# Key pages between the slabs of a two-layer decoder step, scored in groups of four units

## The chip, the cores and the metric

The kernel runs on one core of one Trainium2 chip. The metric is the device time of one launch in microseconds. The kernel before was run three times.

## The reference

One inference step of a two-layer decoder for a prompt group (256 tokens) and a sample group (8 sequences, one new token each, with 2048 cached tokens in pages of 128). Per layer: one input projection, attention over the own tokens or the cache (12 heads) and over 256 memory tokens (4 heads), an output projection, a layer norm, a mixture of 16 experts, and another layer norm. All of it is in float32.

```python
def dsa_sample(q, k_new, v_new, qi, ki_new, wi, pool_k, pool_v, pool_ki, page_table, slopes):   # layer 0
    ki_all = concat(pool_ki[page_table], ki_new)
    sc = indexer_scores(qi, wi, ki_all)
    _, sel = lax.top_k(sc, 256)                      # the 256 best of 2049 positions
    return sparse_attend(q, k[sel], v[sel], pos_q, sel, slopes)

def fox_sample(q, k_new, v_new, logf_new, pool_k, pool_v, pool_lf, page_table):                 # layer 1
    c = cumsum(concat(pool_lf[page_table], logf_new))
    return fox_attend(q, all keys, all values, c)    # softmax(q k + c_q - c_k) v

def mem_attend(qm, mk, mv):                          # 4 heads, 256 memory tokens, both layers
    return softmax(qm mk^T / sqrt(128)) mv
```

The outputs are the new token rows of both groups and the new keys, values, index keys and forget gates.

## The kernel before

Tokens stand transposed: X holds 16 chunks of 128 features by 264 tokens. A **slab** (TensorE, L678 to L699) is a product of X, or of the transposed memory rows AT, with 512 weight columns: two weight units, 64 matmuls, four PSUM banks. Slabs alternate between banks 0 to 3 and 4 to 7; ScalarE copies the four banks out (`slab`, L1540), and the next slab on the same banks waits for that (`slab_copied`). A slab may have small work beside it: `beside(x)` is called after each four matmuls, x from 0 to 15. So `turn_memory` (L668) turns the 16 chunks of the memory rows, two per call from x = 1 on, through banks 4 to 7; at x = 1 it waits until the slab before has been copied, and each chunk waits until the one four before it has been copied by ScalarE (`turn_rows`, L1534). `own_rows` turns new keys and values into rows (`natural`, L701) for the outputs and, in layer 1, the forget gates; `query_blocks` (L736) spreads the sample queries.

**The ring.** Weights, cache pages and memory tokens go through six SBUF units of 2 MB (128 x 4096 floats). `plan(layer)` (L169) is the list of what is loaded in which order; SP walks it (L476), waits for each unit until its last user has freed it (`free`), and issues the DMAs. A weight unit is one DMA (L463). A key or value unit is pages: `load_pages` (L398 to L405) loads eight page numbers into registers and issues one DMA a page: in layer 0 a unit is one sequence, 16 pages of 128 KB; in layer 1 it is half a sequence, 8 pages of 256 KB. There are 8 key units in layer 0 and 16 in layer 1, and as many value units. In the plan all key units come behind all slabs, then mk (memory keys), v, mv, r (router), o (output weights).

**The keys.** VectorE turns each key unit in 32 x 32 blocks in place (`turn_keys`, L2066). TensorE then takes the products of a group of units (`sample_scores`, L906; the matmul is L925): for each key head and each 32 of its features d, for each unit, for each row quarter r, one matmul of 32 x 32 weights with the unit's 32 columns of every page. The PSUM column group is the sequence's number modulo 4, so a group of four sequences uses 16 tiles of the array, a group of two uses 8. Layer 0 has two groups of four units, layer 1 eight groups of two. A float32 matmul is two records in the trace. Behind the groups come the new key (L946), in layer 0 the mask of the top-k as a product (L939, L940), and then the memory keys (L971, L956), whose 16 turned blocks ScalarE copies one by one (`sample_scores`, L1673) with two banks between them.

**VectorE in layer 0:** `sample_topk` (L2019) does 32 rounds of MAX8 and MATCH_REPLACE8 over 2049 scores, writes the mask (L2024), then the 8 key transposes, `new_keys` (which waits for `memory_done`, set by ScalarE after the memory values), `prompt_topk` of block 0, the sample softmax, `prompt_topk` of block 1.

**ScalarE's queue** is in program order too, and it issues DMAs itself: in layer 0 the index pages (`load_ik`), in layer 1 the forget-gate pages, 128 of them, four times 32 (`load_lf`, L1912), between the copies of the first slabs:

```python
for k in range(3):
    if layer == 1 and k == 1: gate_rows(a)
    if layer == 1: load_lf(range(2 * k, 2 * k + 2))
    slab(layer, "q", k, ...)
if layer == 1:
    load_lf(range(6, NB)); slab(layer, "kv", 0, ...)
turn_rows(Ac, 4)
```

The order of slabs is q0, q1, q2 (queries), in layer 1 kv0 (keys), then kv (layer 0: keys and values; layer 1: values) with the memory rows beside it, qm (memory queries) with own rows beside it, mkv0 and mkv1 (memory keys and values, from AT), and then the last rows and the keys. After it: attention, output mixing (L1178), layer norm, experts (L1352 to L1440).

Of the kernel before, what the change touches and what calls it, by code (L numbers as in the profile page):

```python
# [28 lines left out]
ALU = mybir.AluOpType  # L29
# [38 lines left out]
IK_EARLY = 6  # L68

# [82 lines left out]
class Ring:  # L152
# [7 lines left out]
    def take(self, n_dma=1):  # L160
        s = self.n % RING
        self.n += 1
        before = self.used[s]
        self.full[s] += 16 * n_dma
        self.used[s] += 1
        return s, self.full[s], self.used[s], before


def plan(layer):  # L169

    u = []
    if layer == 0:
        u += [("x", 0, 3), ("x", 1, 1), ("x", 2, 1), ("x", 3, 1), ("kiwi", 0, 1)]
        u += [("qi", k, 1) for k in range(2)] + [("ln", 0, 4)] + [("qi", k, 1) for k in range(2, 4)] + [("ik", 0, 16 * (NB - IK_EARLY))]
    else:
        u += [("f", 0, 1)]
    u += [("q", k, 2 if layer == 0 and k == 3 else 1) for k in range(6)]
    if layer == 1:
        u += [("kv", k, 1) for k in range(2)]
    u += [("mem", 0, 1)] + [("kv", 2 * layer + k, 1) for k in range(2)]  # L180
    u += [("qm", k, 1) for k in range(2)] + [("mkv", k, 1) for k in range(4)]
    n = 8 if layer == 0 else 16
    u += [("k", k, 128 // n) for k in range(n)] + [("mk", k, 4) for k in range(2)]
    u += [("v", k, 128 // n) for k in range(n)] + [("mv", k, 4) for k in range(2)]
    u += [("r", 0, 5)] + [("o", k, 1) for k in range(8)]
    return u


def step_kernel(nc, i, o):

    with ExitStack() as ctx:
# [41 lines left out]
        for layer in range(2):  # L233
# [28 lines left out]
            a.KN = a.KTs  # L262
            a.qiT = work[:, 1024:1024 + 8 * T]
# [95 lines left out]
        for layer in range(2):  # L359
# [3 lines left out]
            for name, k, n in plan(layer):  # L363
                at_l[name, k] = r.take(n)
# [42 lines left out]
        def key_unit(layer, u):  # L407
# [3 lines left out]
            return 2 * (u // 4) + u % 2, 8 * (u // 2 % 2), PAGES // 2  # L411

        def key_base(layer):
            return 9 * layer

# [25 lines left out]
        def _(sp):  # L441
# [23 lines left out]
            for layer in range(2):  # L465
# [10 lines left out]
                for name, k, n_dma in plan(layer):  # L476
# [45 lines left out]
                    elif name == "k":  # L522

                        b, first, per = key_unit(layer, k)
                        pages(full(layer, s), b, first, per, ck, lambda g: t[:, (g - first) * W:(g - first + 1) * W])
                    elif name == "v":
                        per = UNIT // W
                        b, first = divmod(k * per, PAGES)
                        pages(full(layer, s), b, first, per, cv, lambda g: t[:, (g - first) * W:(g - first + 1) * W])
# [106 lines left out]
        def _(pe):  # L636
# [6 lines left out]
            def release(layer, name, k=0):  # L643

                leave(pe.transpose(B[4 - (name == "mem")][0:32, 0:32], ident[0:32, 0:32], ident[0:32, 0:32]), layer, name, k)
# [1929 lines left out]
```

## Time and profile before

| what | value |
|---|---|
| median of 3 runs | 2241.7 us (2241.44 to 2243.01) |
| the profiled execution | 2249.78 us |
| its span, first to last instruction | 2248.0 us |
| TensorE busy | 2126.4 us, 95% |
| VectorE, ScalarE, GpSimd busy | 769.5, 387.2, 8.2 us |
| mean granted TensorE clock | 0.97 of full |
| HBM traffic over the span | 639.62 MB read, 5.96 MB written |

Times inside the profile are microseconds from the first instruction. A group of instructions is named by its line, engine and tiles (out<-in); "x128" counts records. "Idle before" is how long the engine stood idle ahead of it, with what ended the idleness; "issue" stands for nothing that the profile shows. PE is TensorE, DVE VectorE, ACT ScalarE, and ACTq or SPq a DMA issued by that engine's queue.

### The profile page before, as it was taken

The numbers are of one execution on the slowest core, as the hardware profiler recorded it, in microseconds if no ns is written. First come the engines' busy times: TensorE is split into PE (matmuls) and PEld (weight loads), VectorE is DVE, ScalarE is ACT, GpSimd is POOL, SyncE is SP. The second block draws the span as 40 slices with busy tenths as digits, with TensorE's granted clock in tenths as the row PEclk, the third lists the DMA queues.
The fourth block names the chain that finished last, engine by engine and source line by source line (L and its number), as shares of the span: only waits on it lengthen the run. The fifth ranks groups of instructions, "written<-read, shape, count | busy, mean of one in ns | idle before, by whom it ended". The sixth has DMA issues, their size and how long they took to land.

```text
span 2248.0 us, 34894 instructions
## 1 busy us (share of the span) xinstructions
PE 2126.4 (95%) x13909; PEld 1321.0 (59%) x13909; DVE 769.5 (34%) x1262; ACT 387.2 (17%) x932; POOL 8.2 (0%) x11
## 2 busy tenths in 40 slices
PE   8999995899999999999899997799999999999999
PEld 7778873578843435353488885445787444443534
DVE  0249966601572222212500044623016622222223
ACT  1221101410330101011310210033104211010112
POOL 0000000000000000000000000000000000000000
PEclk9999997989999999999999999989999999999999
DMA  9743557794359999999945447998742699999994
GB/s 273 229 150 113 197 176 233 207 345 150 113 216 424 414 430 418 428 420 426 375 155 160 167 172 259 372 345 275 251 149 77 275 426 416 427 415 429 414 417 182
DMA packets 213862, 647.49 MB, mean 288 GB/s; under 512 B 55400, under 2 KB 88953, under 8 KB 184161
## 3 DMA queue, kind: packets, MB, share of 16 engines
q1 hardware_dynamic: 180673, 637.39, 73.6%
q10 hardware_dynamic: 33056, 8.27, 1.9%
q8 instruction: 91, 1.49, 0.3%
q14 instruction: 42, 0.34, 0.0%
HBM read 639.62 MB, written 5.96 MB: 287 GB/s over the span
## 4 chain that ended last, share of the span: by engine, by line
PE 80%; DMA 10%; SPq 5%; issue 2%; ACT 1%; DVE 1%; DVEq 0%
PE bank L692 22%; PE bank L1379 14%; PE bank L1178 10%; PE bank L1426 8%; PE bank L1440 6%; DMA ring<-in_w_down 5%; DMA ring<-in_w_up 4%; SPq L405 4%; PE bank L1352 4%; PE bank L925 2%; PE bank L1055 2%; PE bank L1262 1%; PE bank L1036 1%; SPq L402 1%; PE bank L816 1%
## 5 line engine op out<-in xcount | busy, mean ns | idle before, releaser
L1379 PE MATMUL bank<-ring,AT 128*64 128x512 f32 x2048 | 457.3, 596 | 10.8 <-DMA ring<-in_w_up 8.8
L692 PE MATMUL bank<-X,ring 128*128 128x264 f32 x1664 | 385.7, 389 | 6.2 <-ACT X L1777 6.2
L692 PEld LDWEIGHTS bank<-X,ring 128*128 128x128 f32 x1664 | 312.3, 191 | 64.2 <-issue 13.3
L1379 PEld LDWEIGHTS bank<-ring,AT 128*64 128x64 f32 x2048 | 142.4, 137 | 286.4 <-issue 271.4
L1528 ACT ACTIVATE arena<-bank 128x512 f32<-128x512 f32 (+11 forms) x311 | 137.8, 479 | 715.3 <-PE bank L1426 211.3
L1426 PE MATMUL bank<-ring,arena 128*64 128x512 f32 x1024 | 226.5, 598 | 22.3 <-ACT arena L1528 14.7
L2456 DVE TENSOR_TENSOR X<-bank,X 128x264 f32<-128x264 f32 x256 | 110.8, 433 | 367.7 <-PE bank L1440 365.8
L1178 PE MATMUL bank<-AT,ring 128*128 128x264 f32 x1024 | 233.1, 391 | 0.0
L1178 PEld LDWEIGHTS bank<-AT,ring 128*128 128x128 f32 x1024 | 197.1, 193 | 34.3
L1426 PEld LDWEIGHTS bank<-ring,arena 128*64 128x64 f32 x1024 | 76.9, 137 | 161.6 <-issue 158.9
L1528 ACT ACTIVATE AT<-bank 128x512 f32<-128x512 f32 (+3 forms) x176 | 81.9, 489 | 418.8 <-PE bank L1352 194.9
L1440 PE MATMUL bank<-arena 128*128 128x264 f32 x512 | 138.8, 402 | 0.0
L2066 DVE STREAM_TRANSPOSE ring<-ring 128x4096 f32<-128x4096 f32 x24 | 106.3, 4438 | 93.0 <-DMA ring<-in_cache_b_k 64.6
L925 PE MATMUL bank<-ring,arena 32*32 32x256 f32 (+1 forms) x2560 | 85.6, 458 | 51.6 <-DVE ring L2066 32.5
L1440 PEld LDWEIGHTS bank<-arena 128*128 128x128 f32 x512 | 89.0, 189 | 70.0 <-DVE X L2456 46.7
L692 PE MATMUL bank<-AT,ring 128*128 128x256 f32 x512 | 112.0, 379 | 0.0
L692 PEld LDWEIGHTS bank<-AT,ring 128*128 128x128 f32 x512 | 96.8, 190 | 13.2
L925 PEld LDWEIGHTS bank<-ring,arena 32*32 32x32 f32 x2560 | 53.5, 112 | 82.7 <-DVE ring L2066 34.8
L1998 DVE MAX8 arena<-arena 8x8 f32<-8x2049 f32 (+1 forms) x48 | 79.9, 1664 | 42.9 <-ACT arena L1528 41.3
L1352 PE MATMUL bank<-arena 128*128 128x256 bf16 x768 | 89.5, 273 | 0.0
L1352 PEld LDWEIGHTS bank<-arena 128*128 128x128 bf16 x768 | 74.3, 98 | 13.8 <-issue 2.1
L1999 DVE MATCH_REPLACE8 arena<-arena 8x2049 f32<-8x2049 f32 (+1 forms) x48 | 79.1, 1647 | 0.0
(347 smaller groups left out, 1356.7 us busy)
## 6 DMA issues: line engine op xcount, KB each, us to landing
ring<-in_w_gate SPq DMA_DIRECT2D x64, 2048.0 KB, 16.8
ring<-in_w_up SPq DMA_DIRECT2D x48, 2048.0 KB, 15.5
ring<-in_w_down SPq DMA_DIRECT2D x48, 2048.0 KB, 13.2
ring<-in_w_o SPq DMA_DIRECT2D x16, 2048.0 KB, 11.7
ring<-in_w_up SPq DMA_DIRECT2D x32, 1024.0 KB, 7.7
ring<-in_w_down SPq DMA_DIRECT2D x32, 1024.0 KB, 15.7
ring<-in_cache_b_k SPq DMA_DIRECT2D x128, 256.0 KB, 5.2
ring<-in_cache_b_v SPq DMA_DIRECT2D x128, 256.0 KB, 4.7
```

What stands on the lines that cost most here:

```text
L405: eng.dma_start(dst(g + k), cache[bass.ds(page, 1)].rearrange("a p w -> (a p) w")).then_inc(sem, 16)
L692: mm = pe.matmul(B[4 * (g % 2) + f][:, 0:n_tok], u[:, c * 512 + f * P:c * 512 + (f + 1) * P], src[8 * half + c][:, 0:n_tok], start=(half = ...
L925: mm = pe.matmul(B[r][out, 32 * first:32 * (first + per)], a.Qz[kv // 2][rows, at:at + 32], tile[rows, :, kv * P + 32 * d:kv * P + 32 * d ...
L1178: mm = pe.matmul(B[bank0 + f][:, 0:T], u[:, c * 512 + f * P:c * 512 + (f + 1) * P], Ac[8 * half + c], start=(half == 0 and c == 0), stop=( ...
L1352: mm = pe.matmul(B[GATHER_BANKS[q]][:, c * 2 * P:(c + 1) * 2 * P], M.part[t][k][:, at:at + P], M.sel[:, t * 2 * P:(t + 1) * 2 * P], start= ...
L1379: mm = pe.matmul(B[bank][64 * s:64 * s + 64, :], M.xsT[:, at:at + 64], ring[slots[s][0]][:, c * FE:(c + 1) * FE], start=(half == 0 and c = ...
L1426: mm = pe.matmul(B[2 + q][64 * s:64 * s + 64, :], M.hT[:, at:at + 64], ring[slots[s][0]][:, j * D + q * 512:j * D + (q + 1) * 512], start= ...
L1440: pe.matmul(B[2 + c % 4][:, 0:T], M.ys[:, c * P:(c + 1) * P], M.gt[a], start=True, stop=True).then_inc(sm("scattered"), 1)
L1528: return act.activation(out, in_, ACT.Copy, scale=scale)
L1998: link(dve.max(m8, sc))
L2066: dve.transpose(t[:, :], t[:, :]).then_inc(S("keys_made"), 1)
L2456: dve.tensor_tensor(Xc[c], B[2 + c % 4][:, 0:T], Xc[c], ALU.add).then_inc(sm("scatter_added"), 1)
```

## The change

The key units move between the slabs. TensorE's order becomes, in layer 0: q0, q1, q2, kv, qm, key group 0 (units 0 to 3), mkv0, mkv1, key group 1 (units 4 to 7), late rows; in layer 1: q0, q1, kv1 (values, memory rows beside it), q2, kv0 (keys), group 0, qm, group 1, mkv0, group 2, mkv1, group 3, late rows. Groups have four units in both layers; in layer 1 a group is half the pages of four sequences. Key scores stand in banks 0 to 3 in layer 0 and 4 to 7 in layer 1, and slabs beside them use the other four, so each slab names its banks (`at`). The ring's plan can name a slot, which skips some. Slab waits are for the last slab on the same banks.

In layer 0 ScalarE issues the second eight pages of every key unit (`second_pages`), and the second eight of value units 0 to 3, two pages behind each of the 16 memory-key copies. SP issues the first eight. VectorE puts six of the eight key transposes of layer 0 between rounds of the top-k, and `new_keys` behind the first prompt top-k. The rows of the memory keys and values (in layer 1 of the new keys as well) are turned behind the last group, through four banks.

```diff
+TURNS_AFTER = [10, 12, 15, 18, 24, 26]
+SHARED_V = 4
 def plan(layer):
+        u += units("q", range(3)) + units("q", [3], 2) + units("q", range(4, 6))
+        u += units("mem", [0]) + units("kv", range(2))
+        u += units("k", range(3), 16) + units("qm", [0], 1, 0) + units("k", [3], 16, 5) + units("qm", [1], 1, 1)
+        u += units("mkv", range(2), 1, 0) + units("k", range(4, 6), 16) + units("mkv", range(2, 4), 1, 0)
+        u += units("k", range(6, 8), 16, 4) + units("mk", range(2), 4)
+        u += units("v", range(8), 16) + units("mv", range(2), 4)
     else:
+        u = units("f", [0]) + units("q", range(4)) + units("kv", range(2, 4)) + units("mem", [0])
+        u += units("q", range(4, 6)) + units("kv", range(2)) + units("k", range(4), 8)
+        u += units("qm", range(2)) + units("k", range(4, 8), 8)
+        u += units("mkv", range(2)) + units("k", range(8, 12), 8)
+        u += units("mkv", range(2, 4)) + units("k", range(12, 16), 8) + units("mk", range(2), 4)
...
+            def key_products(layer, a, group):
+                us = range(4 * group, 4 * group + 4)
+                if group == 0:
+                    pe.wait_ge(S("q_padded"), (8, 25)[layer])
+                pe.wait_ge(S("keys_made"), key_base(layer) + us[-1] + 1)
...
@@ TensorE's order
+                    slab(layer, "q", 1, Xc, T, 0)
+                    slab(layer, "q", 2, Xc, T, 4)
+                    slab(layer, "kv", 0, Xc, T, 0, lambda x: turn_memory(layer, x))
+                    slab(layer, "qm", 0, Xc, T, 4, own)
+                    key_products(layer, a, 0)
+                    slab(layer, "mkv", 0, Ac, SEQ, 4)
+                    slab(layer, "mkv", 1, Ac, SEQ, 4)
+                    key_products(layer, a, 1)
                 else:
+                    slab(layer, "q", 1, Xc, T, 4, lambda x: gate_rows(a, x))
+                    slab(layer, "kv", 1, Xc, T, 0, lambda x: turn_memory(layer, x))
+                    slab(layer, "q", 2, Xc, T, 4, lambda x: own_rows(layer, a, x, (a.vT,)))
+                    slab(layer, "kv", 0, Xc, T, 0, gates_and_blocks)
+                    key_products(layer, a, 0)
+                    slab(layer, "qm", 0, Xc, T, 0)
+                    key_products(layer, a, 1)
+                    slab(layer, "mkv", 0, Ac, SEQ, 0)
+                    key_products(layer, a, 2)
+                    slab(layer, "mkv", 1, Ac, SEQ, 0)
+                    key_products(layer, a, 3)
+                late_rows(layer, a)
...
@@ ScalarE: memory keys
                 for m in range(2 * NB):
+                    copy(a.KTm[m % 4], B[other + m % 2][:, :]).then_inc(S("km_copied"), 1)
+                    if layer == 0:
+                        second_pages("v", m // 4, 8 + 2 * (m % 4), 2)
...
+            def second_pages(name, k, first=PAGES // 2, n=PAGES // 2):
+                s, _, _, before = units[0][name, k]
+                act.wait_ge(free(0, s), before)
+                load_pages(act, pregs, full(0, s), k, first, n, cache, lambda g: ring[s][:, g * 256:(g + 1) * 256])
...
@@ ScalarE's order
+                if layer == 0:
+                    queries(0, 4)
+                    queries(1, 0)
+                    second_pages("k", 0)
+                    queries(2, 4)
+                    second_pages("k", 1)
+                    second_pages("k", 2)
+                    turn_rows(Ac, 4)
+                    slab(layer, "kv", 0, heads(a.kT, 2) + heads(a.vT, 2), T, 0)
+                    second_pages("k", 3)
+                    key_rows(0)
+                    value_rows(0)
+                    pad_queries(layer, a)
+                    slab(layer, "qm", 0, heads(a.qmT, 4), T, 4, SCALE)
+                    for u in range(4, 8):
+                        second_pages("k", u)
+                else:
+                    load_lf(range(0, 2))
+                    queries(0, 0)
+                    gate_rows(a)
+                    load_lf(range(2, 4))
+                    queries(1, 4)
+                    load_lf(range(4, 6))
+                    turn_rows(Ac, 4)
+                    slab(layer, "kv", 1, heads(a.vT, 4), T, 0)
+                    load_lf(range(6, NB))
+                    value_rows(0)
+                    queries(2, 4)
...
@@ VectorE
+                for u, n in enumerate(TURNS_AFTER):
+                    top_k(sc, a.m8[0:NB, :], 8 * (n - done))
+                    done = n
+                    turn_keys(0, [u])
+                top_k(sc, a.m8[0:NB, :], TOPK_S - 8 * done)
...
-                    turn_keys(layer, range(8))
+                    turn_keys(layer, range(len(TURNS_AFTER), 8))
+                    prompt_topk(a, 0)
                     new_keys(layer, a)
-                    prompt_topk(a, 0)
                 else:
                     forget_gates(a)
+                    turn_keys(layer, range(4))
                     cached_gates(a)
-                    turn_keys(layer, range(16))
+                    turn_keys(layer, range(4, 16))
```

In attention the banks are named by layer, and TensorE's first two prompt scores and first two turns no longer wait for the copies of the turned sample scores.

## Rows read from the trace of the kernel before

**Rows 1.** The page, busy time of TensorE and the instruction queue
```profile
PE 2126.4 (95%) x13909; PEld 1321.0 (59%) x13909; DVE 769.5 (34%) x1262; ACT 387.2 (17%) x932; POOL 8.2 (0%) x11
...
q8 instruction: 91, 1.49, 0.3%
```

**Rows 2.** Busy time by window (us, busy and count per engine, PEclk, DMA share, GB/s)
```profile
325.40:374.30 48.90, 23.53 (x525) 13.11 (x526) 22.66 (x35) 0.29 (x2) 0.95 (x1) 0.74 0.74 239
...
1117.00:1361.90 244.90, 242.87 (x1186) 205.85 (x1186) 37.17 (x22) 35.78 (x101) 4.08 (x3) 0.99 0.51 167
1361.90:1453.40 91.50, 66.72 (x2049) 42.90 (x2049) 50.48 (x20) 0.26 (x1) 0.95 (x1) 0.91 0.94 335
```

**Rows 3.** Timeline of TensorE, layer 0 (start, us, what, [idle before <-releaser])
```profile
325.48 8.69 PE L925 MATMUL bank<-ring,arena 32*32 32x512 f32 x256 [0.80 <-ACT arena L1528]
359.46 10.15 PE L925 MATMUL bank<-ring,arena 32*32 32x512 f32 x256 [25.29 <-DVE ring L2066]
...
374.23 3.77 PE L971 MATMUL bank<-consts,ring 128*128 128x128 f32 x16
```

**Rows 4.** Waits, 320 to 480 us (waiter, releaser: us, times, longest)
```profile
PE bank L1055 <- DMA ring<-in_cache_a_v: 6.4, 3, 3.6
```

**Rows 5.** Timeline of TensorE, attention of layer 0
```profile
452.20 1.94 PE L1055 MATMUL bank<-ring,arena 128*32 128x256 f32 x16 [3.57 <-DMA ring<-in_cache_a_v]
```

**Rows 6.** Instruction groups, 1361.9 to 1453.4 us (busy, mean ns, idle before)
```profile
L925 PE MATMUL bank<-ring,arena 32*32 32x256 f32 x2048 | 66.7, 412 | 25.5 <-issue 17.6 <-DVE ring L2066 7.2 <-ACT arena L1528 0.7
```

**Rows 7.** Timeline of TensorE, key groups of layer 1
```profile
1370.18 11.84 PE L925 MATMUL bank<-ring,arena 32*32 32x256 f32 x384 [2.90 <-issue]
...
1394.67 9.87 PE L925 MATMUL bank<-ring,arena 32*32 32x256 f32 x256 [4.41 <-DVE ring L2066]
...
1439.67 3.69 PE L925 MATMUL bank<-ring,arena 32*32 32x256 f32 x128 [2.82 <-issue]
1445.90 3.69 PE L925 MATMUL bank<-ring,arena 32*32 32x256 f32 x128 [2.55 <-issue]
```

**Rows 8.** Timeline of ScalarE, page loads in both layers
```profile
60.00 0.66 ACT L1581 ACTIVATE arena<-bank 128x256 f32<-128x256 f32 x2 [3.73 <-PE bank L793]
60.48 1.86 ACTq L405 DMA_DIRECT2D arena<-in_cache_a_ik  x4
...
1197.14 17.79 ACTq L405 DMA_DIRECT2D arena<-in_cache_b_lf  x31
```

**Rows 9.** Timeline of ScalarE, copies out of slabs of layer 0
```profile
203.08 1.24 ACT L1528 ACTIVATE arena<-bank 128x264 f32<-128x264 f32 x4 [27.24 <-PE bank L692]
...
265.20 1.24 ACT L1528 ACTIVATE arena<-bank 128x264 f32<-128x264 f32 x4 [13.87 <-PE bank L692]
...
322.33 1.21 ACT L1528 ACTIVATE AT<-bank 128x256 f32<-128x256 f32 x4 [20.12 <-PE bank L692]
```

**Rows 10.** Timeline of TensorE, a turned memory chunk (layer 0) and slabs (layer 1)
```profile
210.87 0.60 PE L652 MATMUL bank<-consts,ring 128*128 128x128 f32 x4
...
1173.89 66.13 PE L692 MATMUL bank<-X,ring 128*128 128x264 f32 x296
```

**Rows 11.** Timeline of VectorE, sample top-k and transposes of layer 0
```profile
144.40 2.28 DVE L1998 MAX8 arena<-arena 8x8 f32<-8x2049 f32 x1 [41.28 <-ACT arena L1528]
...
294.68 1.22 DVE L2024 TENSOR_SCALAR arena<-arena 8x2049 f32<-8x2049 f32 x1
...
320.02 4.45 DVE L2066 STREAM_TRANSPOSE ring<-ring 128x4096 f32<-128x4096 f32 x1 [6.80 <-DMA ring<-in_cache_a_k]
```

**Rows 12.** Timeline of ScalarE, first and last of 16 memory-key copies
```profile
375.39 0.60 ACT L1528 ACTIVATE AT<-bank 128x512 f32<-128x512 f32 x1 [48.19 <-PE bank L971]
...
389.74 1.08 ACT L1528 ACTIVATE AT<-bank 128x512 f32<-128x512 f32 x2 [0.51 <-PE bank L971]
```

**Rows 13.** Timeline of ScalarE, forget-gate pages of layer 1
```profile
1176.33 19.43 ACTq L405 DMA_DIRECT2D arena<-in_cache_b_lf  x32
...
1196.64 0.41 ACT L1528 ACTIVATE arena<-bank 128x264 f32<-128x264 f32 x1
```

More of the change, by code:

```diff
@@ L262, in step_kernel @@
             a.KN = a.KTs
+            a.MN = work[:, 1024:2048]
             a.qiT = work[:, 1024:1024 + 8 * T]
@@ L362, in step_kernel @@
             at_l = {}
-            for name, k, n in plan(layer):
-                at_l[name, k] = r.take(n)
+            for name, k, n, slot in plan(layer):
+                at_l[name, k] = r.take(n, slot)
             units.append(at_l)
@@ L524, in _ @@
                         b, first, per = key_unit(layer, k)
-                        pages(full(layer, s), b, first, per, ck, lambda g: t[:, (g - first) * W:(g - first + 1) * W])
+                        pages(full(layer, s), b, first, 8, ck, lambda g: t[:, (g - first) * W:(g - first + 1) * W])
                     elif name == "v":
@@ L759, in indexer, with late_rows @@
+            def late_rows(layer, a):
+                pe.wait_ge(S("slab_copied"), cnt["slab"])
+                at = other_banks(layer)
+                if layer == 1:
+                    for t in range(3):
+                        natural(a.kT, a.nk, t, at)
+                for src in (a.memK, a.mvT):
+                    for t in range(2):
+                        natural(src, HM, t, at, SEQ)
+                pe.wait_ge(S("natural_copied"), cnt["natural"])
             def indexer(a):
@@ L934, in cached_mask @@
+            def sample_scores(layer, a):
+                bank, other = key_banks(layer), other_banks(layer)
                 def cached_mask(a):
@@ L989, in attention @@
                 per = UNIT // a.W
+                bank, other = key_banks(layer), other_banks(layer)
                 def scores(n):
@@ L1675, in sample_scores @@
                 base = layer * KM_STEPS
+                bank, other = key_banks(layer), other_banks(layer)
                 pad_memory_queries(layer, a)
@@ L1695, in attention @@
                 nm, rs = a.st[:, 0:6], a.st[:, 6:12]
+                bank, other = key_banks(layer), other_banks(layer)
                 def ov_copy(x):
@@ L2084, in sample_softmax @@
                 nm, rs = a.st[:, 8:10], a.st[:, 10:12]
+                bank, other = key_banks(layer), other_banks(layer)
                 S_ = a.S[:, 0:L1]
```

321 lines of the change are left out of this document (148 added, 173 removed).

## The prediction, made before the changed kernel was run

> **What bounds the kernel now.** The page comes first: TensorE is busy 95% of the span [rows 1], so time comes off only where it waits, where its clock is low, or where it works more slowly than it could. The stretches by window show where that is: at the sample keys of each layer. In layer 0 it is the 48.9 us from the first key group to the end of the mask products, with 23.5 us of matmul in them and a granted clock of 0.74 of full; in layer 1 it is 91.5 us of key products alone [rows 2]. The dense stretch of layer 1 ahead of them is full (242.9 of 244.9 us). The timeline of layer 0 has 8.69 us of products, 25.29 us of waiting for VectorE's transposes, and 10.15 us of products, then new key and mask until 374.23 [rows 3]. The list of waits adds 6.4 us on value pages in attention [rows 4], the longest of them 3.57 us, with slow matmuls behind it [rows 5]. In layer 1 the groups show 66.7 us of products, 7.2 us of waiting for keys and 17.6 us put down to "issue" [rows 6]: a run of 128 records lasts 3.69 us, and the next starts 6.2 us after it started [rows 7]. I read this as code that comes late. The instruction queue moved 1.49 MB in 91 packets [rows 1], 16 KB each. I take one packet to carry one such run, 128 matmul records and their 128 weight loads, 64 bytes each.
>
> **Layer 0, up to the key scores.** ScalarE's queue gets 8 page loads for each of eight key units. In the old page loads 31 take 17.79 us [rows 8], 0.57 each, so 8 cost 4.6 us. Those of k1 and k2 (9.3 us) start when query slab 2 is copied out, at 204.3 [rows 9], and end at 213.6. The first copy of a turned memory row, which TensorE wants at 210.87 [rows 10], then comes at 214: +3.2 us. Those of k0 and k3 to k7 lie beside slabs. The two memory slabs now use the same four banks, one behind the other, so the second waits for the first's copies (four, 1.21 us, as the last of rows 9): +1.4 us. SP loads the qm units and the last mkv units only when a unit is freed in the middle of a slab, 14 us before they are wanted, where the mkv loads took 8.2 us to land (the page's list of issues). I take 0, bounds 0 and 5.
>
> VectorE runs its 32 rounds from 144.40 to 294.68, 4.70 us each; six transposes of 4.45 us [rows 11] now stand among them. k1 is wanted after 12 rounds and one transpose, at 205.2, and lands at 211: +5.8. k4 can load only when the first group has freed its place, at 278.3 (slab qm ends at 265.0 in rows 9, +3.2, query blocks 0.8, group 9.3); it lands at 285.3 and is wanted at 280.9: +4.4. So the eighth transpose ends at 144.4 + 150.3 + 26.7 + 10.2 + 1.2 (mask) + 8.9 (k6 and k7) = 341.7. TensorE is through its slabs at 322.3 + 3.2 + 1.4 + 9.3 = 336.2 and waits 5.5 us instead of 25.3. Then come 10.2 for the second group, 3.5 for the late rows, and 4.7 for new key and mask: 360.1 instead of 374.2, **14.1 us earlier**. VectorE's prompt top-k and new-key products, 10.2 us, cost nothing because group and late rows (13.7) cover them; without that cover it would be their 10.2 us, and 3.5 us are spare.
>
> **Layer 0, memory keys and attention.** ScalarE gets 32 value pages, two behind each of its 16 copies, and TensorE waits on those copies. A relu with four pages behind it ran from 60.00 to 62.34 [rows 8]; less two pages at 0.47 that is 1.4 us, so 1.45 for a copy with two pages. 15 steps, the exp of 2.0 between them and the last copy make 24.3 us, against 15.4 now (375.39 to 390.82 [rows 12]): +8.9. Of the 14.1 us, **5.2** are left when attention starts. There the value pages now lead (SP issues half of v0 to v3, and starts when the second group ends, at 352 instead of 369.6). The 6.4 us of waits [rows 4] go, and a little of the slow matmuls: **7 us**, bounds 3 and 9. Layer 0: -12.2 us.
>
> **Layer 1, ahead of the keys.** The value slab, with the memory rows turned beside it, is now third instead of fifth. ScalarE still has its forget-gate pages between the copies: 32 from 1176.33 to 1195.8, the copy of slab 2 until 1197.05, 32 more until 1214.9, and only then a copy again [rows 8, 13]. Slab 2 ends at 1179.2 (24 of 296 records from 1173.89 on [rows 10]). Before, nobody wanted these copies soon. Now the third slab's first memory turn, 3.6 us in, waits for slab 2's copy, 1182.8 to 1197.05. Four turned chunks later, 4.4 us, it needs the first of them copied out of its bank, and that copy stands behind the next 32 pages, until 1215.3. Queued behind TensorE's waits is the rest of the slab. Delay: 1215.3 - (1179.2 + 3.6 + 4.4) = 28.1, and 2.5 for a slow start, as in the 256 records of 9.87 us behind 4.41 us idle, where two runs of 3.69 are 7.4 [rows 7]. **+30.6 us**, and nothing hides it: TensorE is the full engine here.
>
> **Layer 1, the key groups.** The 2048 records stay, now in four groups of 512, each behind a slab. The pages of a group start when the group before it ends; 32 pages at about 0.6 us and one transpose, 24 us, lie under a slab of 28.5 us. So the waits for keys (7.2) go; late by 5 us each, they would cost 15. Four units instead of two address 16 tiles of the array instead of 8. No row has 256 columns on 16 tiles. Lower end: half of 66.7, 33 us with no gap. Upper end: 66.7 + 17.6 = 84 us. My value: of the four code blocks of a group the first is there and takes 1.9 us at doubled pace; the other three come at the mean of 3.9 (11.84 us for 384 records without a gap) and 6.2 [rows 7], with some relief because no pages move, 4.9 us. That is 16.6 a group, **66 us against 91.4: -25.4**. It is nearest to the rows with gaps, because code and not streaming sets the pace. Five transposes of 0.43 us leave the slabs and come back behind them: 0. Layer 1: +5.2 us.
>
> **Sum.** -12.2 + 5.2 = -7.0. The profiled execution took 2249.8 us (span 2248.0 and 1.8 around it), 8.1 above the median of the runs, 2241.7. Set against the median: 2234.7. Mixing and experts issue the same instructions, and their loads move along.
>
> **A rule weighed.** [Rows 7] show TensorE idle for 2.5 to 2.9 us after runs of 128 records. The Trainium skill, Runtime: NRT & Kernel Launch, section Instruction fetch mechanics, says that code is streamed in 16 KiB blocks, the next while one executes, and that this is hidden under issue. The trace disagrees in this stretch. By that rule the groups would cost what the products alone do.
>
> **Rivals.** (1) *Code keeps up.* Few pages move while a group runs, and 384 records did pass without a gap [rows 7]. Groups of 10.5 us, 42 in all: layer 1 is 30.6 - 49.4 = -18.8, the total -31.0, 2210.7. Against it: each group starts just as SP issues a 2 MB weight half. (By the Trainium skill's section above this would be the outcome.) (2) *ScalarE's queue decides, slower.* Its place is the third slab of layer 1, its price 30.6. With groups of G in all the change is -12.2 + 30.6 - (91.4 - G): above zero from G = 73.0, slower by 0.2% from 77.5. At 84 it is +11.0, 2252.7. For it: the pages and copies of [rows 13] are unchanged and the new order puts the waits behind them. (3) *Keys late in layer 0.* The transposes wait more among the rounds or weight halves land late; 341.7 becomes 350, layer 0 gains 4 instead of 12.2, and the total is +1.2, 2242.9. That the change does not do what it says is no case: all orders are written out.
>
> **Chances.** Forecast 0.42 (2227 to 2243), code keeps up 0.22, ScalarE decides 0.21, late keys 0.15. A measurement of this kernel can tell about 0.2%, 4.5 us, from no change. Faster by more: rival 1 and most of the forecast, 0.60. Within it: 0.19. Slower: 0.21. The range, 2208 to 2256, takes in groups from about 40 to 84 us and leaves out 2 in 10.
>
> **What would show it.** Right: about 5 us of waiting for keys in layer 0; memory keys about 25 us long, with page issues between ScalarE's copies; no wait for value pages; two TensorE waits of about 14 us in layer 1's third slab, ended by ScalarE; key groups of 15 to 18 us with issue gaps. Wrong: groups of 10 us or less; a third slab without a stall; mask products of layer 0 no earlier than before.

## The result and the profile after

The change made the kernel **slower by 0.27%**. The median is 2248.8 us (20 runs, 2239.3 to 2257.5), beside 2242.7 us (20 runs, 2234.4 to 2247.0) of the kernel before on the same chips, a ratio of 1.0027 with a 95% interval of 1.0014 to 1.0040, about 6 us. The forecast was 2234.7 and faster; the time lies in the range, on the other side. The profiled execution took 2252.6 us (span 2250.7), 2.7 more than that of before (2248.0). A single execution strays by up to 0.4% from its median, so the 2.7 is what the two traces can account for and the other 3 us of the medians are not in them.

The page of the changed kernel, the lines that answer to [rows 1]: the same instructions, the same code packets (PEld is TensorE loading weights).
```profile
PE 2117.5 (94%) x13909; PEld 1316.5 (58%) x13909; DVE 768.9 (34%) x1262; ACT 387.0 (17%) x932; POOL 8.2 (0%) x11
...
q8 instruction: 91, 1.49, 0.3%
```
I cut both spans at the same events on TensorE: the first transpose of a memory key, the first attention scores, the first mixing product, the first slab of layer 1. Start times before and after, and what each stage gained or lost:

| stage, up to | before | after | stage |
|---|---|---|---|
| layer 0: key scores made, first memory-key transpose | 374.2 | 365.0 | -9.2 |
| memory keys, to the first scores | 395.0 | 395.4 | +9.7 |
| attention, to the first mixing product | 474.6 | 466.4 | -8.6 |
| mixing and experts (no edit in them), to layer 1 | 1117.0 | 1106.0 | -2.8 |
| layer 1: slabs and key groups, to the first memory-key transpose | 1453.6 | 1455.7 | +13.1 |
| the rest | 2248.0 | 2250.7 | +0.6 |

Layer 0 gave what was forecast less 4 us, layer 1 cost 8 more. The -2.8 is noise: in the profiles of the ten experiments, whose code is the same there, this stage took 641.4 to 644.6 us, and 639.7 in this one. So the part that the change touches is +5 us in the traces (-8.1 and +13.1), close to the 6 of the medians.

**Layer 0.** TensorE's timeline, answering to [rows 3] (start, us, what, idle before and what ended it). Between the two memory slabs and the second group stands the wait for keys, now 8.2 us instead of 25.3; the products behind that idleness take 10.43 us for 256 records, at a mean granted clock of 0.81 of full (0.50, the level of 1.2 GHz, until about 350.5, then 1.00, the level of 2.4 GHz).
```profile
281.55 27.89 PE L717 MATMUL bank<-AT,ring 128*128 128x256 f32 x128
310.74 27.89 PE L717 MATMUL bank<-AT,ring 128*128 128x256 f32 x128 [1.30 <-ACT arena L1570]
346.86 10.43 PE L947 MATMUL bank<-ring,arena 32*32 32x512 f32 x256 [8.22 <-DVE ring L2150]
...
360.67 0.38 PE L968 MATMUL bank<-consts,AT 128*128 128x1 f32 x2 [1.49 <-ACT arena L1570]
```
VectorE's timeline shows where it is made: the transpose of k1 waits 7.8 us for its pages, and that of k4 7.1. Both queues start on k4's pages at 281.4, when the first group has freed the place, and the transpose can start 9.3 us later.
```profile
213.53 4.45 DVE L2150 STREAM_TRANSPOSE ring<-ring 128x4096 f32<-128x4096 f32 x1 [7.78 <-DMA ring<-in_cache_a_k]
...
290.69 4.45 DVE L2150 STREAM_TRANSPOSE ring<-ring 128x4096 f32<-128x4096 f32 x1 [7.14 <-DMA ring<-in_cache_a_k]
```

**Layer 1, the third slab.** TensorE's timeline of it. Before, all of the dense stretch had 2 us of idle time [rows 2]; now there are two holes in this slab, 12.85 and 11.23 us, and the first products behind each are slow (3.58 and 3.15 us for 8 records instead of 1.95): the granted clock was 0.56 of full from 1186.2 to 1191.0 and 0.61 from 1204.1 to 1208.4, which is the level of 1.2 GHz (0.50) for most of each stretch, and 1.00, 2.4 GHz, from 1208.4 on.
```profile
1186.19 1.12 PE L671 MATMUL bank<-consts,ring 128*128 128x128 f32 x4 [12.85 <-ACT arena L1570]
1187.10 3.58 PE L717 MATMUL bank<-X,ring 128*128 128x264 f32 x8
...
1204.13 1.12 PE L671 MATMUL bank<-consts,ring 128*128 128x128 f32 x4 [11.23 <-ACT AT L1570]
1205.04 3.15 PE L717 MATMUL bank<-X,ring 128*128 128x264 f32 x8
1208.02 0.60 PE L671 MATMUL bank<-consts,ring 128*128 128x128 f32 x4
1208.46 1.95 PE L717 MATMUL bank<-X,ring 128*128 128x264 f32 x8
```
ScalarE's timeline says what it did meanwhile (ACTq is its queue, issuing transfers): 32 forget-gate pages, four copies with a page among them, 31 more pages, and only then the copies that TensorE stood for.
```profile
1166.61 18.24 ACTq L414 DMA_DIRECT2D arena<-in_cache_b_lf  x32
1184.90 0.95 ACT L1570 ACTIVATE arena<-bank 128x264 f32<-128x264 f32 x3 [20.31 <-issue]
1185.71 0.34 ACTq L414 DMA_DIRECT2D arena<-in_cache_b_lf  x1
1185.73 0.41 ACT L1570 ACTIVATE arena<-bank 128x264 f32<-128x264 f32 x1
1186.21 17.43 ACTq L414 DMA_DIRECT2D arena<-in_cache_b_lf  x31
1203.69 1.97 ACT L1570 ACTIVATE AT<-bank 128x256 f32<-128x256 f32 x6 [17.56 <-issue]
```

**Layer 1, the key groups.** TensorE's timeline of the third and the fourth, answering to [rows 7]. A run of 128 records takes 2.74 us instead of 3.69 and starts 3.5 to 4.0 us after the one before instead of 6.2. Three of the four groups begin with a wait for VectorE's transposes.
```profile
1385.52 5.71 PE L947 MATMUL bank<-ring,arena 32*32 32x256 f32 x209 [3.26 <-DVE ring L2150]
1392.18 2.74 PE L947 MATMUL bank<-ring,arena 32*32 32x256 f32 x128 [0.95 <-issue]
1396.20 2.74 PE L947 MATMUL bank<-ring,arena 32*32 32x256 f32 x128 [1.27 <-issue]
1399.67 1.35 PE L947 MATMUL bank<-ring,arena 32*32 32x256 f32 x47 [0.73 <-issue]
1400.94 27.89 PE L717 MATMUL bank<-AT,ring 128*128 128x256 f32 x128
1432.74 5.89 PE L947 MATMUL bank<-ring,arena 32*32 32x256 f32 x209 [3.90 <-DVE ring L2150]
```
The list of TensorE's waits from 1110 to 1460 us (in total, times, longest) holds all that layer 1's part has but 0.6 us: the gaps in the groups, the stall in two rows, the keys, and a wait behind the late rows.
```profile
PE bank L947 <- issue: 15.6, 11, 3.4
PE bank L671 <- ACT arena L1570: 12.9, 1, 12.9
PE bank L671 <- ACT AT L1570: 11.2, 1, 11.2
PE bank L947 <- DVE ring L2150: 8.9, 3, 3.9
PE bank L968 <- ACT arena L1570: 2.6, 1, 2.6
```
The four groups, from the end of the slab ahead to their last product, take 16.2, 18.2, 18.7 and 20.3 us: 73.3 in all, 8.9 of it waiting for keys, 15.6 in gaps, and 48.8 of products; 64.4 without the key waits.

### The profile page after: what moved, and what is told of

Read it like the earlier page. It is cut to its first block, busy times and chain, and to the rows that moved or that the text cites. A ratio compares the mean times of both kernels' runs of the same rounds, so it can differ in the third digit from the quotient of the medians.

```text
span 2250.7 us, 34920 instructions
## 1 busy us (share of the span) xinstructions
PE 2117.5 (94%) x13909; PEld 1316.5 (58%) x13909; DVE 768.9 (34%) x1262; ACT 387.0 (17%) x932; POOL 8.2 (0%) x11
## 4 chain that ended last, share of the span: by engine, by line
PE 77%; DMA 10%; DVE 4%; ACTq 3%; issue 2%; SPq 2%; ACT 2%; DVEq 0%
PE bank L717 15%; PE bank L1398 14%; PE bank L1197 10%; PE bank L1445 8%; PE bank L1459 6%; DMA ring<-in_w_down 5%; DMA ring<-in_w_up 4%; PE bank L1371 4%; PE bank L947 3%; PE bank L1074 2%; ACTq L414 2%; SPq L414 2%; DVE ring L2150 1%; PE bank L1055 1%; DMA ring<-in_cache_b_k 1%
## 5 line engine op out<-in xcount | busy, mean ns | idle before, releaser
L717 PE MATMUL bank<-X,ring 128*128 128x264 f32 x1664 | 391.4, 393 | 6.2 <-ACT X L1823 6.2
L2541 DVE TENSOR_TENSOR X<-bank,X 128x264 f32<-128x264 f32 x256 | 110.8, 433 | 367.3 <-PE bank L1459 365.4
L947 PE MATMUL bank<-ring,arena 32*32 32x256 f32 (+1 forms) x2560 | 69.3, 466 | 33.6 <-DVE ring L2150 17.1
L947 PEld LDWEIGHTS bank<-ring,arena 32*32 32x32 f32 x2560 | 44.4, 108 | 57.0 <-issue 28.2
```

What stands on the lines that cost most here:

```text
L717: mm = pe.matmul(B[at + f][:, 0:n_tok], u[:, c * 512 + f * P:c * 512 + (f + 1) * P], src[8 * half + c][:, 0:n_tok], start=(half == 0 and c ...
L947: mm = pe.matmul(B[bank + r][out, 32 * first:32 * (first + per)], a.Qz[kv // 2][rows, at:at + 32], tile[rows, :, kv * P + 32 * d:kv * P + ...
L2541: dve.tensor_tensor(Xc[c], B[2 + c % 4][:, 0:T], Xc[c], ALU.add).then_inc(sm("scatter_added"), 1)
```

## The experiments

Each kernel ran 6 to 12 times on the same chip as 17 to 30 runs of the kernel before; ratios are to those. "Changed" is the changed kernel, 1.0027. The stages of its profile, against which the traces of the experiments are read: layer 0's key scores ready at 365.0, memory keys 30.4 us, attention 71.0, layer 1 up to its memory keys 349.7.

| run | ratio, 95% interval | median us | stage that it touches |
|---|---|---|---|
| gate pages spread | 0.9925, 0.9903 to 0.9947 | 2222.6 | layer 1: 322.1 |
| value pages by SP | 1.0022, 1.0003 to 1.0041 | 2245.1 | memory keys 18.3, attention 77.3 |
| shorter keys | 0.9992, 0.9973 to 1.0011 | 2240.6 | layer 1: 340.5 |
| pairs | 1.0017, 0.9997 to 1.0037 | 2243.3 | layer 1: 346.2 |
| half the columns | 1.0019, 0.9997 to 1.0042 | 2248.2 | layer 1: 348.8 |
| spread + pairs | 0.9887, 0.9862 to 0.9913 | 2220.7 | layer 1: 319.2 |
| spread + pairs + k1 early | 0.9833, 0.9809 to 0.9857 | 2206.4 | scores ready at 355.6 (before this edit 365.4) |
| spread + pairs + two value units | 0.9876, 0.9846 to 0.9905 | 2216.8 | memory keys 26.6, attention 71.0 |
| k1 early alone | 0.9980, 0.9960 to 1.0000 | 2237.8 | scores ready at 356.8 |
| all four edits | 0.9849, 0.9819 to 0.9878 | 2207.2 | memory keys 25.1, attention 71.0 |

**Gate pages spread.** The forget-gate pages leave their places between the copies of the second and third slab; one sequence's go two by two behind every second copy of a turned memory chunk (the function given to `turn_rows` is called after each copy; its definition is left out here).
```diff
                     queries(0, 0)
+                    load_lf([2])
                     gate_rows(a)
-                    load_lf(range(2, 4))
                     queries(1, 4)
-                    load_lf(range(4, 6))
-                    turn_rows(Ac, 4)
+                    turn_rows(Ac, 4, lambda c: c % 2 and lf_pages(3, c - 1, 2))
+                    load_lf([4])
                     slab(layer, "kv", 1, heads(a.vT, 4), T, 0)
-                    load_lf(range(6, NB))
+                    load_lf(range(5, NB))
```


> Only the order of ScalarE's queue in layer 1 is changed: the copies of the three slabs no longer stand behind 32 forget-gate pages each, but behind 16 at most, and one sequence's pages go two by two between the copies of turned memory rows. Theory (ScalarE's pages are what stalls TensorE in the third slab, and nothing takes the stall's place): the two waits of 12.9 and 11.2 us go but for 2 us or so, and the kernel is 24 to 28 us faster than the changed kernel, about 2222 us, 20 faster than the kernel before. Rival A (the loss is given back later): the key transposes and the memory keys wait instead, and less than 8 us come off. Rival B (copies with two pages between them are too slow for the turned rows, 1.45 us each against a chunk of the slab of 1.8): waits of 0.5 us or more at each chunk, and about half of it, 12 us, comes off.

Measured: 2222.6 us, layer 1's stage 27.6 us shorter. TensorE's timeline, same place: no wait in the third slab, and a granted clock of 1.00 from 1171.1 to 1190.7, although pages stand between the copies.
```profile
1171.08 0.60 PE L671 MATMUL bank<-consts,ring 128*128 128x128 f32 x4
1171.51 1.95 PE L717 MATMUL bank<-X,ring 128*128 128x264 f32 x8
...
1187.05 3.73 PE L717 MATMUL bank<-X,ring 128*128 128x264 f32 x16
```
The last 47 pages cost 1.8 us of waiting two slabs later, and the key waits stay as they were (8.8 us in three). So the stall was the pages' and next to nothing took its place. Both rivals fall. With this edit added the change makes the kernel 0.75% faster.

**Value pages by SP.** `SHARED_V = 0`, and ScalarE's call for them goes:
```diff
-                    if layer == 0:
-                        second_pages("v", m // 4, 8 + 2 * (m % 4), 2)
```


> SP issues all value pages of layer 0 and ScalarE none, the rest as in the changed kernel. Theory (the 32 pages between ScalarE's 16 copies cost the memory keys 9 us): from the first memory-key transpose to the first scores about 21 us instead of 30.4, so 9 us come off there. Then attention decides: if SP alone is quick enough, the start of mixing is 9 us earlier, about 2240 us in all; the rival (value pages late as in the kernel before) has 4 to 8 us of waits on value pages return, and a total within 4 us of the changed kernel.

The memory keys fell by 12.1 us, more than expected (ScalarE's copies are 0.8 us apart instead of 1.6), and attention rose by 6.3, with the value waits back:
```profile
PE bank L1074 <- DMA ring<-in_cache_a_v: 3.6, 3, 2.2
```
Those waits are 3.6 us, just under the 4 to 8 of the rival; the total can't be told from the changed kernel's, as the rival has it. (Its key scores came at 368.4, in code that is the same; over the profiles that instant spreads from 362.7 to 368.4.)

**Shorter keys.** In layer 1 half of the units beyond the first group load 4 pages of 8; the scores of the pages left out are made from what lay there. (The plan's page counts change with it; left out here.)
```diff
-                        pages(full(layer, s), b, first, 8, ck, ...
+                        half = layer == 1 and k > 3 and k % 4 > 1
+                        pages(full(layer, s), b, first, 4 if half else 8, ck, ...
```


> In layer 1 the last two of four key units of groups two to four load only 4 of their 8 pages (the sample's other pages there are left out, so this computes something else); 24 pages instead of 32 a group. Theory (SP's pages for a group, at 0.66 us each after a start of 9 us, are 2 to 5 us longer than the slab that covers them): the waits of 1.7, 3.3 and 3.9 us ahead of the key products go, and 9 us come off, with groups of 16 us each. Rival (the waits are VectorE's turn, not the pages'): they stay within 1 us, and nothing comes off.

No wait for keys is left, layer 1's stage is 9.2 us shorter, and the total is 0.35% below the changed kernel's, which is even with the kernel before. The theory holds. TensorE's timeline at the second group; the slab ahead ends at 1338.4:
```profile
1309.63 28.75 PE L719 MATMUL bank<-X,ring 128*128 128x264 f32 x128
1338.31 4.53 PE L949 MATMUL bank<-ring,arena 32*32 32x256 f32 x210
1346.01 6.67 PE L949 MATMUL bank<-ring,arena 32*32 32x256 f32 x256 [3.17 <-issue]
```

**Pairs.** Layer 1's groups of four scored as two pairs.
```diff
...
+                if layer == 1 and len(us) == 4:
+                    for us in (us[0:2], us[2:4]):
+                        key_products(layer, a, group, us)
+                    return
```


> Layer 1's four groups of four key units are scored as two pairs each, 8 tiles of the array at once instead of 16; everything else is in the order of the changed kernel. Theory (128 records with their loads set the pace, 21.5 ns a record while code is there, so four tiles more at a time give little by themselves): a pair of 256 records takes 8 to 9 us as in the kernel before (8.3 of products and gaps on average), a group 17 us, and the total moves by less than 4 us. Rival (addressing 16 tiles is what brought a group down from 22.9 us to 16 to 18): a group takes 21 us or more, and the total is 12 to 18 us slower than the changed kernel.

The groups took 17.4, 17.3, 18.0 and 17.6 us, 70.3 in all: 5.9 more of products, 8.9 less of waiting, because the first pair's places come free halfway and their pages start then (SP's first at 1303.9, 7.3 us before the group ends; in the changed kernel it starts when the group has ended). The products take 58.7 us instead of 48.8, the gaps 11.6 instead of 15.6:
```profile
1339.94 6.01 PE L951 MATMUL bank<-ring,arena 32*32 32x256 f32 x209
1347.52 3.53 PE L951 MATMUL bank<-ring,arena 32*32 32x256 f32 x128 [1.57 <-issue]
1351.25 3.68 PE L951 MATMUL bank<-ring,arena 32*32 32x256 f32 x128 [0.20 <-issue]
```
So of what the key products lost without their waits (84.2 us before, 64.4 after), not more than 5.9 is the wider address on the array. The other 13.9 came with pairs too: it belongs to the place behind the slabs. Two things are different there. The first 210 or so records of every group pass without a gap, and behind them the DMA engines are nearly idle. The busy time by window (start and end, length, busy time and count of TensorE, its loads, VectorE, ScalarE and GpSimd, granted clock, DMA share, GB/s), from the start of one run of 128 records to the start of the next: one of the changed kernel, two in a row of this one, and one of the kernel before:
```profile
1392.18:1396.20 4.02, 2.74 (x129) 1.85 (x128) 0.00 (x0) 0.00 (x0) 0.00 (x0) 1.00 0.01 4
...
1347.52:1351.25 3.73, 3.53 (x128) 2.73 (x128) 0.00 (x0) 0.00 (x0) 0.00 (x0) 1.00 0.17 23
1351.25:1355.83 4.58, 3.69 (x129) 2.36 (x129) 0.00 (x0) 0.00 (x0) 0.00 (x0) 1.00 0.94 312
...
1439.67:1445.90 6.23, 3.68 (x128) 2.50 (x128) 0.90 (x5) 0.00 (x0) 0.00 (x0) 1.00 1.00 362
```
In the changed kernel such a step takes 3.5 to 4.0 us at a DMA share of 0.01 or 0.02. With pairs it takes 3.7 to 4.0 us at 0.15 to 0.19, and 4.3 to 4.6 in the second half of a group, where the next pages already move, at 0.91 to 1.01. In the kernel before, the steps with a gap take 4.9 to 6.5 us at 0.88 to 1.05. So the pace gets slower when the DMA engines are full. By this, about 2.4 of the 5.9 us are the pages' (an estimate: the four last steps of the pairs against the four before them), and the address on the array is at most the rest.

**Half the columns.** Each key product of layer 1 reads 128 columns; half of the scores are left out.
```diff
+                n = per if layer == 0 else per // 2
...
-                                               tile[rows, :, kv * P + 32 * d:kv * P + 32 * d + 32],
+                                               tile[rows, 0:n, kv * P + 32 * d:kv * P + 32 * d + 32],
```


> Every key product of layer 1 reads 128 columns of the keys instead of 256, with the same number of instructions; the scores of half of each unit's pages are left out. Theory (in the groups the pace is that of the instructions, not of the columns that stream): a run of 128 records starts 3.5 to 4.0 us after the one before, as with 256 columns, and a group without key waits still takes 15 to 16.5 us. Rival (the streaming of 256 columns on 16 tiles sets the pace, the gaps are a queue that fills): a run starts within 2.5 us of the one before, and a group takes 8 to 11 us.

TensorE's timeline of the second group. The first 210 records take 3.04 us instead of 4.53, and the gap behind them grows from 3.2 to 4.1 us; the group takes 15.6, and the four 63.3 (64.4 with 256 columns).
```profile
1340.05 3.04 PE L948 MATMUL bank<-ring,arena 32*32 32x128 f32 x210
1347.15 2.59 PE L948 MATMUL bank<-ring,arena 32*32 32x128 f32 x128 [4.06 <-issue]
1350.88 2.81 PE L948 MATMUL bank<-ring,arena 32*32 32x128 f32 x128 [1.15 <-issue]
1354.36 1.38 PE L948 MATMUL bank<-ring,arena 32*32 32x128 f32 x46 [0.66 <-issue]
```
The steps between the later runs are still 3.5 to 3.8 us, but they don't test the columns. The window of one of them shows the granted clock at 0.50 of full (1.2 GHz); 128 columns took 2.81 us a run there, as long as 256 at 1.00 (2.75):
```profile
1350.88:1354.36 3.48, 2.81 (x128) 2.13 (x128) 0.00 (x0) 0.00 (x0) 0.00 (x0) 0.50 0.02 5
```
The test is ahead of them. In the first two groups the first 210 records ran at 1.00, as with 256 columns, and were through 1.5 us earlier; yet the next run starts 7.1 and 7.2 us after the group does. With 256 columns and the same clock it is 7.7 and 8.0 in the changed kernel, and 6.9 to 7.7 in the other runs with 16 tiles. Two more readings agree. In the changed kernel's first group the clock is 0.75 behind the gap, 256 records take 6.66 us instead of 5.5, and the steps are still 3.5 us. With pairs a run takes 3.5 us instead of 2.75, and the steps at a nearly idle DMA are still 3.7 to 4.0.

So the theory holds: the pace is the instructions', at least 3.5 us for each 128 records and their loads, and streaming hides in it. That they wait for code to be fetched is argued, from the packet count [rows 1], from gaps that come back every 128 records, and from a pace that falls when the DMA engines are full; it is not shown. A limit on issuing, for the 3.5 us with the DMA engines idle, is a rival that no run tested: none changed how code arrives.

The total did not fall with the groups, because the granted clock did. It was 0.70 and 0.74 of full over the first two groups and 0.93 to 0.96 in the slabs behind the first three, against 0.89, 1.00 and 1.00 in the changed kernel. The three slabs took 30.8, 29.0 and 29.3 us instead of 28.7, 27.9 and 27.9, and the longer cover left 3.9 us of key waits instead of 8.9.

**Spread and pairs together.**

> Two edits together in layer 1: ScalarE's forget-gate pages spread as in the first experiment, and the groups of four units scored as two pairs each. Theory (the third slab's stall and the key waits are separate prices): the stall's 26 to 28 us and the waits' 9 us go, pairs cost 5.9 us more of products, so 2 to 4 us less than with the pages spread alone: about 2219 us. Rival (the key waits only move): the same as with the pages spread alone, 2222 us.

2220.7 us, ratio 0.9887. Layer 1's stage is 319.2 us, 2.9 less than with the pages spread alone, as expected, and no key wait is in it. The ratios of the two, from different batches, have overlapping intervals, so the total doesn't show the 2.9.

**And k1 early.** In layer 0:
```diff
-TURNS_AFTER = [10, 12, 15, 18, 24, 26]
+TURNS_AFTER = [10, 12, 15, 18, 27, 29]
...
                     second_pages("k", 0)
+                    second_pages("k", 1)
                     queries(2, 4)
-                    second_pages("k", 1)
                     second_pages("k", 2)
```


> The edits of the run before, and in layer 0 ScalarE issues k1's eight pages before the third query slab is copied instead of after it, and VectorE turns the last two units of the second group after rounds 27 and 29 instead of 24 and 26. Theory (VectorE's 7.8 us wait for k1 is passed on to TensorE's 8.2 us wait for the last keys): VectorE's wait for k1 falls below 2 us, TensorE waits 2 to 4 us for keys, and layer 0's key scores end 5 us earlier; 2 of the 5 or more reach the end. Rival (transposes are held up by k4 and the mask anyway): TensorE's wait changes by less than 2 us and nothing reaches the end.

The key scores are ready 9.8 us earlier, twice the expected. The median falls by 14 us; in the traces layer 1 starts 10.0 us earlier, and the rest lies in stages whose code is the same. VectorE's timeline: the second transpose waits for nothing, the fourth waits 4.2 us, and the fifth, moved behind later rounds, for nothing. TensorE waits 1.2 us for keys (2 to 4 were expected), the 2.3 us for memory rows are gone, since eight pages instead of sixteen stand ahead of the copies, and the group runs at a granted clock of 1.00 (6.48 and 3.24 us for 256 records).
```profile
206.19 4.45 DVE L2159 STREAM_TRANSPOSE ring<-ring 128x4096 f32<-128x4096 f32 x1
...
247.18 4.45 DVE L2159 STREAM_TRANSPOSE ring<-ring 128x4096 f32<-128x4096 f32 x1 [4.19 <-DMA ring<-in_cache_a_k]
```
```profile
335.86 6.48 PE L951 MATMUL bank<-ring,arena 32*32 32x512 f32 x180 [1.19 <-DVE ring L2159]
342.90 3.24 PE L951 MATMUL bank<-ring,arena 32*32 32x512 f32 x76 [0.56 <-issue]
```

**k1 early alone**, on the changed kernel:

> The changed kernel with one edit in layer 0 alone: ScalarE issues k1's eight pages before it copies the third query slab, and VectorE turns the last two units of the second group after rounds 27 and 29. Theory (the wait is one chain: k1 late, VectorE's transposes late, TensorE's second group late): 9 to 12 us less than the changed kernel, as between the two runs before that differ by it, so 2237 to 2240 us, faster than the kernel before by 0.1 to 0.3%. Rival (that difference came from the other edits beside it): 2246 us or more.

Ratio 0.9980, 0.47% below the changed kernel's, about 10 us: the theory holds. This edit would just have given the change the forecast sign; the interval ends at 1.0000. It has two parts, k1's pages and the rounds of the last transposes, and no run separates them.

**Two value units shared instead of four**, on spread and pairs (the "second run" of the text below):
```diff
-SHARED_V = 4
+SHARED_V = 2
...
-                    if layer == 0:
+                    if layer == 0 and m < 8:
                         second_pages("v", m // 4, 8 + 2 * (m % 4), 2)
```


> The edits of the second run, and in layer 0 ScalarE shares the pages of two value units instead of four with SP (16 pages between its copies, not 32). Theory (the 9.7 us that the memory keys gained are 32 pages at 0.3 us, and attention's gain of 8 us comes mostly from the first value pages): the memory keys are 4 to 6 us shorter than with 32, and attention not more than 2 us longer: 3 us less in all. Rival (each page that SP takes over comes back as a value wait): attention is 4 us longer, and the total unchanged.

The memory keys are 2.5 us shorter, less than expected, and attention is not longer (71.0 us against 73.5). The ratios, 0.9876 and 0.9887, can't be told apart.

**All four edits.**

> All four edits together: forget-gate pages spread, groups scored as pairs in layer 1, k1 issued early with the later last transposes, and value pages of two units shared instead of four. Theory (the four prices are separate): 2202 to 2206 us, 1.75 to 1.9% faster than the kernel before. Rival (earlier memory keys only make attention wait for value pages): 2206 to 2208 us, the same as without the last edit.

2207.2 us, ratio 0.9849: no better than the 0.9833 with four value units shared. The rival holds in the total, although not as it said: attention (71.0 us) has no value wait, and the memory keys are 5.8 us shorter in the trace. In the trace 8 us come back in layer 1 from its memory keys on, where the two kernels have the same code, so it is spread between executions; the intervals, 0.3% to each side, don't show 5 us. Both versions beat both kernels; the better measured one is that with the first three edits, 1.7% faster than the kernel before.

## Why the prediction was wrong

The mechanisms were there, each where it was forecast; two terms of the sum were too favourable. **The step that failed is the one on layer 1's key pages**: "32 pages at about 0.6 us and one transpose, 24 us, lie under a slab of 28.5 us. So the waits for keys (7.2) go". They came to 8.9 us instead of 0. The step priced the pages by SP's issue, and SP did issue 32 in 19.8 us; but the first land late, and the rest not at that pace. VectorE's transposes of the changed kernel, whose waits end with the pages, show the delivery:
```profile
1316.72 4.45 DVE L2150 STREAM_TRANSPOSE ring<-ring 128x4096 f32<-128x4096 f32 x1 [37.02 <-DMA ring<-in_cache_b_k]
1322.57 4.45 DVE L2150 STREAM_TRANSPOSE ring<-ring 128x4096 f32<-128x4096 f32 x1 [1.40 <-DMA ring<-in_cache_b_k]
1327.95 4.45 DVE L2150 STREAM_TRANSPOSE ring<-ring 128x4096 f32<-128x4096 f32 x1 [0.94 <-DMA ring<-in_cache_b_k]
1333.37 4.45 DVE L2150 STREAM_TRANSPOSE ring<-ring 128x4096 f32<-128x4096 f32 x1 [0.97 <-DMA ring<-in_cache_b_k]
```
SP starts at 1307.7; the first unit can be turned 9.1 us later, the next ones 5.4 to 5.9 us apart (2 MB in 5.4 us is 388 GB/s, at a DMA share of 1.00), the last at 1333.4, and it is done at 1337.8: 30.2 us behind a group whose slab lasts 28.7. Of the 6 us beyond the 24, about 4 are the start (9.1 us until the first eight are there, 5.0 to issue them) and 2 the slower pace. For the third and the fourth group it is 30.9 and 31.5 us, under slabs of 27.9. The run with fewer pages took the waits away and 0.35% off; the pairs did the same by an earlier start. The prediction had the price ("late by 5 us each, they would cost 15") and gave it no weight in the sum.

This step alone doesn't turn the sign: without its 8.9 us the kernel is even with the one before (shorter keys, 0.9992), not 7 us faster. The rest is layer 0's term, 4 us short, and part of it is the same mistake: k4's unit was given 7 us from the first issue to its use, and took 9.3.

The other steps, in its order:
- *Layer 0, to the key scores, -14.1*: -9.2. The chain was right (k1's pages late, VectorE late, TensorE's 8.2 us of waiting instead of 5.5); the waits of VectorE were 7.8 and 7.1 us instead of 5.8 and 4.4, and 0.75 for a third, so the last transpose came 5 us after the 341.7 forecast. The 3.2 us on memory rows were 2.3, the 1.4 between the memory slabs 1.3. With k1 early the scores are ready 17.4 to 18.6 us before the old kernel's 374.2.
- *Memory keys +8.9*: +9.7. *Value waits in attention -7*: -8.6, and no such wait is left. All 32 pages could go back to SP for no loss or gain that the total shows: the two terms are one trade.
- *Third slab of layer 1, +30.6*: the stage fell by 27.6 with the pages spread, and 1.8 of waiting for them was left in it, so 29.4. The two waits of 12.9 and 11.2 (about 14 each were forecast) and the slow start behind each were where they were forecast; the first ended at 1186.2, the second 17.9 us later. Right.
- *Key groups 66 us*: 64.4 without key waits, 73.3 with them. The value between the bounds was right. The prediction began with the four units that address 16 tiles; by the pairs they are at most 5.9 of the 20 us that the products lost, and the place behind the slabs is the rest. Rival 1, 42 us with no gaps, falls: the products alone were 48.8, and the gaps 15.6. By the Trainium skill (Runtime: NRT & Kernel Launch, section Instruction fetch mechanics) the fetch of code is hidden under the issue of instructions, with a floor of about 20 cycles an instruction for that issue, which rival 1's 42 us left out. The gaps of the trace, one behind every 128 records, are more than that rule leaves room for as the prediction read it; whether they are fetch or issue no run here shows.
- *Late rows of layer 1 at 0*: five transposes cost little, but behind them TensorE waits 2.6 us for ScalarE's last copy before the new key. In the kernel before other products covered it.

Rival 2, ScalarE's queue decides, had the sign: it put the break-even at groups of 73.0 us in all, and they took 73.3, which by its sum is +0.3 us. Half of rival 3, keys late in layer 0, came on top: it had layer 0 8 us short, and it was 4. Neither rival alone gives the measured +5. Rival 2 had 0.21; the forecast had twice that, by a sum that took the best value of a term whose bound, 15 us, was twice the gain. Layer 1 came out at +13.1 instead of +5.2, layer 0 at -8.2 instead of -12.2; both errors go the same way, and 12 us of them turn -7.0 into +5 before noise.

## What to carry to other kernels

Price a load by the slower of two rates, the queue's issue and the bytes' delivery, and add the time from the first issue to the first use; then compare the sum with the cover to the microsecond, since a cover that is 5 to 13% too short shows in every round. When the order of one engine is changed, write down for every engine beside it what now stands ahead of the work that the first one needs: here 64 small page issues, harmless for as long as nobody wanted the copies behind them, cost 1% of the kernel. When an expected gain is no larger than one wait that the sum puts at nothing, the forecast is "unclear", whatever the sum says.

## What the runs showed of the hardware

- With 32x32 tiles, 128 matmul records and their 128 weight loads took no less than 3.5 us from start to start: 3.5 to 4.0 us at a DMA share of 0.01 to 0.07, with 256 columns at the full clock as with 128 at half of it, 4.3 to 4.6 at 0.91 to 1.01 in the run with pairs, and 4.9 to 6.5 at 0.88 to 1.05 in the kernel before.
- A run of 128 such records on 16 tiles took 2.74 us and on 8 tiles 3.5 to 3.7. The gaps of the four groups were 15.6 us on 16 tiles and 11.6 on 8, which takes back 4 of the 10 us of products: twice the tiles gave 8% on a group and not half.
- With half the columns in the key groups, the granted clock was 0.70 and 0.74 over the first two groups and 0.93 to 0.96 in the slabs behind instead of 1.00, and the kernel was no faster.
- A queue that issued 256 KB pages every 0.62 us had them delivered every 0.68 us at a DMA share of 1.00, with the first eight ready 9.1 us after the first issue.
